# Twelve post-norms in PSUM, diagonals on ScalarE, and three small reorderings between the layers of a two-block fp32 network

## The reference, cut to what matters

```python
# block 1: stages 0, 1, 2 - the output y is normed ahead of the addition
x = x + 0.5 * rms_norm(swiglu_ffn(rms_norm(x, norm_pre[0]), ...), norm_post[0])
x = x + rms_norm(token_mixer(rms_norm(x, norm_pre[1]), ...), norm_post[1])
x = x + 0.5 * rms_norm(swiglu_ffn(rms_norm(x, norm_pre[2]), ...), norm_post[2])
# block 2: stages 3, 4, 5 - y is added as it is
h = h + 0.5 * swiglu(rms_norm_2(h, ffn1_norm), ...)
h = h + merged @ w_out
h = h + 0.5 * swiglu(rms_norm_2(h, ffn2_norm), ...)
```

## Time and profile before

| | |
|---|---|
| median of three runs | 2366.21 us (2357.22 to 2366.54) |
| the profiled execution | 2365.65 us, of which its span is 2364.3 us |
| TensorE matmuls busy | 2299.1 us |
| TensorE weight loads busy | 1890.1 us |
| GpSimd busy | 1317.9 us |
| VectorE busy | 868.7 us |
| ScalarE busy | 448.2 us |

### The profile page before, as it was taken

How to read it: one execution, slowest core, us unless ns; L and a number is a source line. 1 busy time by engine, 2 the same in 40 slices (tenths; PEclk the granted TensorE clock), 3 DMA queues, 4 the chain that set the end, 5 groups by cost and what they waited for, 6 DMA issues and landing times.

```text
span 2364.3 us, 25758 instructions
## 1 busy us (share of the span) xinstructions
PE 2299.1 (97%) x10888; PEld 1890.1 (80%) x10888; DVE 868.7 (37%) x902; ACT 448.2 (19%) x721; POOL 1317.9 (56%) x772
## 2 busy tenths in 40 slices
PE   8999998999999999999999999999988999999999
PEld 7888887887778888888888888877656788888887
DVE  3333104884234434104543202321567623434013
ACT  3111003323223111003111002011268121111012
POOL 5666664634146666665666665656114656666654
PEclk9999999999799999999999999999899999999999
DMA  4333332211123333332323332233000223333322
GB/s 177 98 98 94 94 97 72 73 53 54 36 80 96 93 98 98 98 98 82 98 95 95 96 98 90 89 92 98 27 1 1 72 89 98 98 96 94 105 89 89
DMA packets 55579, 201.04 MB, mean 85 GB/s; under 512 B 6408, under 2 KB 6536, under 8 KB 55336
## 3 DMA queue, kind: packets, MB, share of 16 engines
q1 hardware_dynamic: 53856, 194.14, 26.6%
q10 hardware_dynamic: 1608, 5.25, 0.6%
HBM read 197.27 MB, written 2.10 MB: 84 GB/s over the span
## 4 chain that ended last, share of the span: by engine, by line
PE 90%; DVE 5%; ACT 3%; issue 2%; POOL 1%; DMA 0%; ACTq 0%; DVEq 0%; POOLq 0%
PE psum L385 19%; PE psum L386 19%; PE psum L387 19%; PE psum L466 7%; PE psum L468 7%; PE psum L467 7%; PE psum L611 1%; DVE x L1722 1%; PE psum L1106 1%; PE psum L666 1%; PE psum L1108 1%; PE psum L1107 1%; PE psum L504 1%; PE psum L948 1%; ACT work L1567 1%
## 5 line engine op out<-in xcount | busy, mean ns | idle before, releaser
L350 POOL TENSOR_TENSOR w_lo<-w_raw,w_hi 128x1024 fp32r<-128x1024 f32 (+1 forms) x365 | 885.7, 2427 | 30.4
L348 POOL TENSOR_SCALAR w_hi<-w_raw 128x1024 fp32r<-128x1024 f32 (+1 forms) x365 | 391.1, 1072 | 889.2 <-PE psum L387 641.9
L385 PE MATMUL psum<-u_hi,w_hi 128*128 128x512 f32 (+1 forms) x2072 | 795.5, 384 | 4.3 <-DVE u_lo L1682 2.2
L386 PE MATMUL psum<-u_hi,w_lo 128*128 128x512 f32 (+1 forms) x2072 | 790.5, 382 | 0.0
L387 PE MATMUL psum<-u_lo,w_hi 128*128 128x512 f32 (+1 forms) x2072 | 790.4, 381 | 0.0
L385 PEld LDWEIGHTS psum<-u_hi,w_hi 128*128 128x128 f32 x2072 | 393.6, 190 | 82.2 <-issue 4.8
L387 PEld LDWEIGHTS psum<-u_lo,w_hi 128*128 128x128 f32 x2072 | 393.5, 190 | 74.4
L386 PEld LDWEIGHTS psum<-u_hi,w_lo 128*128 128x128 f32 x2072 | 393.8, 190 | 73.7 <-issue 0.7
L466 PE MATMUL psum<-w_hi,hidden_hi 128*128 128x512 f32 x800 | 311.7, 390 | 1.0 <-DVE work L1945 1.0
L467 PE MATMUL psum<-w_lo,hidden_hi 128*128 128x512 f32 x800 | 311.2, 389 | 0.0
L468 PE MATMUL psum<-w_hi,hidden_lo 128*128 128x512 f32 x768 | 298.8, 389 | 0.0
(11 more groups left out here) (280 smaller groups left out, 1716.1 us busy)
## 6 DMA issues: line engine op xcount, KB each, us to landing
w_raw<-in_ffn_in SPq DMA_DIRECT2D x176, 512.0 KB, 3.5
w_raw<-in_ffn_out SPq DMA_DIRECT2D x88, 512.0 KB, 3.5
w_raw<-in_proj_in SPq DMA_DIRECT2D x34, 512.0 KB, 3.5
w_raw<-in_mix_in SPq DMA_DIRECT2D x29, 512.0 KB, 3.5
w_raw<-in_embed SPq DMA_DIRECT2D x10, 512.0 KB, 3.6
w_raw<-in_mix_out SPq DMA_DIRECT2D x8, 512.0 KB, 3.5
w_raw<-in_branch SPq DMA_DIRECT2D x8, 512.0 KB, 3.5
w_raw<-in_proj_out SPq DMA_DIRECT2D x8, 512.0 KB, 3.5
```

Source lines behind the costliest of these rows:

```text
L348: pool.tensor_scalar(hi, raw, 1.0, 1.0, ALU.mult, ALU.mult).then_inc(k.w_split, 1)
L350: pool.tensor_tensor(lo, raw, hi.bitcast(F32), ALU.subtract).then_inc(k.w_split, 1)
L385: pe.matmul(out, hi[:, cols], xhi, start=first, stop=False)
L386: pe.matmul(out, lo[:, cols], xhi, start=False, stop=False)
```

## The change

Five things are done.

1. The post writes its product back to the PSUM banks that it read; the update reads PSUM. The two scratch buffers are no longer used there, and the wait on them is gone. Since `y` now lies in PSUM until the update, turning waits for `x_updated` in every stage.
2. In front of the gated mixer ScalarE builds the four diagonals (new `act_diag`); VectorE keeps the inverse.
3. There, VectorE's update 1 moves ahead of tile 0's inverse, and post 2 and update 2 both stand ahead of tile 1's inverse.
4. In stages 4, 5 and 6 ScalarE squares the fourth tile of `x` behind both pairs' roundings.
5. In stage 0 TensorE turns tile 2 ahead of the first chunk.

```diff
 def wait_out_taken(k, eng, st, i):
-    if st < 3:
-        eng.wait_ge(k.t_done, NT * st + i + 1)
-    else:
-        eng.wait_ge(k.x_updated, NT * st + i + 1)
+    eng.wait_ge(k.x_updated, NT * st + i + 1)
...
     pe_turn_tile(k, s, 0)
     pe_turn_tile(k, s, 1)
+    pe_turn_tile(k, s, 2)
     if s == 0:
         pe_dense_half(k, s, name, c0, CHUNK_BANK[0], 0)
-    pe_turn_tile(k, s, 2)
     pe_turn_tile(k, s, 3)
...
+def act_diag(k, i):
+
+    act = k.nc.scalar
+    act.wait_ge(k.x_inv, i + 1)
+    act.activation(k.diag[:, i * P:(i + 1) * P], k.cst(C_ID), ACT.Copy, scale=k.x_r[:, i:i + 1]).then_inc(k.x_diag, 1)
...
         square_y(2)
+        if s not in LATE:
+            act_diag(k, 0)
         square_x(1)
         square_y(3)
+        if s not in LATE:
+            act_diag(k, 1)
         square_x(2)
+        if s not in LATE:
+            act_diag(k, 2)
+            square_x(3)
+            act_diag(k, 3)
     else:
-        for i in range(NT):
+        for i in range(NT - 1):
             square_x(i)
-    if s not in LATE:
-        square_x(3)
     act_hi(k, s, 0)
     act_hi(k, s, 1)
     if s in LATE:
-        if st < 3:
-            square_x(3)
+        square_x(3)
...
     dve.reciprocal(r, r).then_inc(k.x_inv, 1)
-    dve.wait_ge(k.x_inv, i + 1)
-    dve.tensor_scalar(k.diag[:, i * P:(i + 1) * P], k.cst(C_ID), r, None, ALU.mult).then_inc(k.x_diag, 1)
...
-    if i >= 2:
-        dve.wait_ge(k.x_updated, NT * st + i - 1)
-    elif i == 0:
+    if i == 0:
         dve.wait_ge(k.post_loaded, 16 * (st + 1))
     scale = factors(k, st)[:, i:i + 1] if st in LATE else 1.0
-    dve.scalar_tensor_tensor(out=t, in0=y, scalar=scale, in1=k.post[:, :], op0=ALU.mult, op1=ALU.mult).then_inc(k.t_done, 1)
+    dve.scalar_tensor_tensor(out=y, in0=y, scalar=scale, in1=k.post[:, :], op0=ALU.mult, op1=ALU.mult).then_inc(k.t_done, 1)
...
-        dve.scalar_tensor_tensor(out=x, in0=normed_tile(k, i), scalar=r, in1=x, op0=ALU.mult, op1=ALU.add).then_inc(k.x_updated, 1)
+        dve.scalar_tensor_tensor(out=x, in0=out_tile(k, i), scalar=r, in1=x, op0=ALU.mult, op1=ALU.add).then_inc(k.x_updated, 1)
...
         dve_update(k, st, 0)
+        dve_update(k, st, 1)
         if s not in LATE:
             dve_root_x(k, s, 0)
-        dve_update(k, st, 1)
         dve_post(k, st, 2)
+        dve_update(k, st, 2)
         if s not in LATE:
             dve_root_x(k, s, 1)
-        dve_update(k, st, 2)
```

More of the change, by code:

```diff
@@ L1696, in dve_post @@
 def dve_post(k, st, i):
-    dve, t, y = k.nc.vector, normed_tile(k, i), out_tile(k, i)
+    dve, y = k.nc.vector, out_tile(k, i)
     dve.wait_ge(k.y_squared, NT * st + i + 1)
-    if i >= 2:
-        dve.wait_ge(k.x_updated, NT * st + i - 1)
-    elif i == 0:
+    if i == 0:
         dve.wait_ge(k.post_loaded, 16 * (st + 1))
     scale = factors(k, st)[:, i:i + 1] if st in LATE else 1.0
-    dve.scalar_tensor_tensor(out=t, in0=y, scalar=scale, in1=k.post[:, :], op0=ALU.mult, op1=ALU.mult).then_inc(k.t_done, 1)
-def normed_tile(k, i):
-    return k.scf[:, (1 + 2 * (i % 2)) * T:(3 + 2 * (i % 2)) * T]
+    dve.scalar_tensor_tensor(out=y, in0=y, scalar=scale, in1=k.post[:, :], op0=ALU.mult, op1=ALU.mult).then_inc(k.t_done, 1)
 def dve_update(k, st, i):
```

## The result

The changed kernel takes **2345.65 us** (median of 7 executions, 2343.45 to 2346.74). Beside it, seven executions of the kernel before had a median of 2357.22 us (2355.15 to 2366.54). The ratio is 0.9935, with a 95% interval of 0.9918 to 0.9953: 0.65% faster (the means of the seven are 2360.0 and 2345.2). A second set on another chip gave 2345.47 us and 0.9931 [0.9910, 0.9952]. The profiled execution took 2346.0 us, its span 2344.7 us, at a mean granted clock of 0.987. The one before took 2365.65 us, at 0.982.

A forecast was written before the change was run, and what follows sets the result against it. TensorE was held to bound the kernel, so only seams, where it waits for VectorE, could win. Gains of 8.5 + 2.0 + 1.8 + 1.9 + 1.1 = 15.3 us from 2365.65 gave 2350 us, range 2342 to 2362.

The forecast's parts named there:

- the base of the sum: Whole kernel: the profiled execution, 2365.65 us, from which the gains were subtracted, held to lie 0.6 us under the runs' median.
- rival A: Mixers and later work: shifted half-clock stretches eat part of the gain, 5 us, giving 2362 us; chance 0.12.
- better ends: Seams and start: the largest gains allowed for the five terms, 8.8 + 4 + 3 + 2 + 2 us.
- The start: Start of the program: tile 2's eight transposes fit into TensorE's idle 2.23 us, gaining 1.1 us, ends 0 and 2.
- Seam 2: Between stages 1 and 2: update 3 ends sooner, so the first chunk comes 2.0 us earlier, ends 1.1 and 4.
- Seam 1: Ahead of the gated mixer (stage 1): first chunk 8.5 us earlier, low end 5.6 if TensorE drops to half clock.
- Seam 3: Between stages 2 and 3: update 3 ends sooner, so the first chunk comes 1.8 us earlier, ends 0.8 and 3.
- Seams 4, 5, 6: Starts of stages 4, 5 and 6: ScalarE's rounding begins sooner, 3 x 0.6 = 1.9 us as written, ends 1.2 and 2.
- Post in PSUM: VectorE's post at the seams: reading and writing PSUM takes 1.28 us, upper bound 2.56 us, a gain excluded.
- rivals B and C: First three seams: PSUM post takes 2.56 us, giving 2361 us (chance 0.07), or 3.37 us, giving 2371 us (chance 0.03).
- Diagonal on ScalarE: Ahead of the gated mixer: each diagonal built on ScalarE takes 0.3 us, bounds nothing and 0.41 us.
- Rival D: Ahead of the gated mixer: ScalarE's four waits for the inverse cost 1 us each, giving 2354 us; chance 0.08.

The follow-up runs named there:

- e6_in_place_shift: Kernel before with post and update in PSUM alone, plus eight unused matmuls ahead of the attention mixer's 32nd projection chunk: 2356.18 us, ratio 0.9981.
- e8_after_shift: Changed kernel plus eight unused matmuls ahead of the attention mixer's 32nd projection chunk: median 2346.01 us, ratio 0.9940; its traced execution took 2355.97 us.

## Why the prediction was right on the seams and wrong in size

Forecast 2350 us, measured 2345.65: 4.4 us too high. As a gain it is further off: 2350 lies 7.2 us under the median of the kernel before, and 11.6 were measured (the ratio of 0.9935 says 15).

- **The step that failed is the base of the sum**, "the profiled execution lies 0.6 us under the median of the runs". The three executions then known were 2366.21, 2366.54 and 2357.22 us, and their spread of 9 us was given no term. With seven the median is 2357.22, 8.4 us under the profiled execution. Of 91 executions of the kernel before whose clock is on record above, 33 were at 0.982 or 0.983 (2364 to 2367 us), 29 at 0.985 or 0.986 (2358 to 2362) and 29 at 0.987 (2355 to 2358). The sum was subtracted from the slowest of these groups. The trace of the changed kernel lies 19.7 us under that one, with the mixers' half clock alike in both.
- **That the time came near is luck in part.** From the median of 2357.22 the sum of 15.3 would have given 2341.9 us, 3.7 below the measured time. A base 8.4 us too high and a sum above the 11.6 us between the medians went against each other. The medians lie closer than the traces because the median execution of the kernel before has less half clock in it than the traced one, and the changed kernel has stayed within 3.3 us of time.
- **The sum has no term for the mixers.** Against the trace at 0.986 the start, the seams and stages 2 and 3 gave 17.0 us, 1.7 more than the sum, and the mixers took 4.56 back. The prediction has this only as its rival A.
- **The range** names its better ends, 8.8 + 4 + 3 + 2 + 2 = 19.8 us, which give 2345.85 us. The measured time lies 0.2 us below that. The range's lower end of 2342 is nearly 4 us lower still, and no term stands for these.
- **Two terms were too small against the same trace, both by the clock.** The start was taken at 1.1 us and gave 3.0, since a half-clock stretch behind TensorE's idle 2.23 us went away with it. Seam 2 was taken at 2.0: the seam gave 2.50 and the layer behind it 1.84, as the half clock of its first chunks (0.56 us a row, 0.37 after) went away; the prediction had that as its upper end ("the first chunk is faster too", 4 us). It wasn't the wait that decided it, which is as long as before (2.20 us against 2.12); behind a wait of 2.21 us, the kernel `e6_in_place_shift` turned there at half clock, 16 in 3.28 us, and seam and layer together gained 2.7 us there instead of 4.3. These two are 4.2 of the 4.3 us between the sum of 15.3 and the 19.6 of the ledger's left column.
- **Seam 1 was right**: 8.64 measured against the same trace, 8.5 taken (7.67 against the trace at 0.986). The replay's end fits to 0.15 us (first post to chunk 16.85 forecast, 17.00 measured), and update 3 ends 377.25 + 1.29 - 366.05 = 12.5 us behind the first post, as replayed. The full clock held there, which was the better end.
- **Seam 3**: taken 1.8, measured 1.06, and 1.72 with the layer. Update 3 came 2.5 us sooner, as forecast, but TensorE turned at half clock, 16 in 3.17 us. That was the low end, 0.8.
- **Seams 4, 5, 6**: 0.61, 0.55, 0.60, together 1.76. The prediction took 3 x 0.6 and wrote 1.9, which should be 1.8.
- **Post in PSUM**: 1.29 us, taken 1.28. With it rivals B and C fell.
- **Diagonal on ScalarE**: rows of 0.39 us, taken 0.3, bound 0.41. The next instruction starts 0.29 us behind it (372.98 to 373.27), so in the replay 0.3 was the right step. The estimate from the Trainium skill (VectorE: DVE Perf Modes, section on the TRN2 errata), 0.29 us, fits that step and not the row. Rival D fell: ScalarE waited 0.83 and 0.23 us for an inverse, where it had nothing else to do.
- **The dearer PSUM source of the Trainium skill** (VectorE: DVE Perf Modes, same section; 120 cycles against 58) again showed no step: 1283 ns from SBUF without GpSimd beside it, 1283 ns from PSUM.
- **Rival A**, the mixers' clock taking back part, was priced at 5 us with a chance of 0.12. The half-clock stretches it names are real, and differ between executions: they cost the traced execution with the post in PSUM alone 7.65 us in stage 4, and the changed kernel 4.56 against the traces at 0.986. It didn't show against the trace that served as the base, since that had lost as much. That the change itself brings them on is not shown. A half-clock microsecond costs 0.5 us: from 0.9825 to 0.987 of 2360 us are 2 x 0.0045 x 2360 = 21 us at half clock, and the groups lie 10 us apart.

What stays open: why the changed kernel has kept within 3.3 us so far and the kernel before spreads over 12, and what in the mixers decides it. Neither the moment of the start nor 1 to 2 us of work moved it in a way that could be foretold.

## What to carry to other kernels

Before subtracting a sum from a traced execution, see where that execution stands among the others by its mean granted clock. Between two kernels compare stretch by stretch, and first those that the change leaves alone: an equal mean clock doesn't say that they had equal half clock there. An instruction of VectorE with two SBUF inputs took up to 2.1 us more than its 1.28 us beside a busy GpSimd; leaving one operand in PSUM took that away and cost 9 ns. Give each seam a term of its own for the half clock that may stand behind it: it was worth 1.7 us at the start and 1.8 in the layer behind seam 2, as much as the work removed.

## What the runs showed of the hardware

- A VectorE instruction that reads and writes the same PSUM banks costs 1292 ns for 128x1024, against 1284 into SBUF.
- The contention goes both ways: beside the long update GpSimd's rounding took 2.02 us, in seam 1 of the changed kernel, beside VectorE's PSUM forms, 1.04 to 1.05. A 128x128 product takes VectorE 0.29 us alone and up to 1.90 beside GpSimd.
- The same program on the same chip has several levels of time, 2355 to 2367 us. The traces at 2358 and 2366 us differ by half-clock stretches inside work that is otherwise the same. The mean granted clock of an execution, 0.982 to 0.987 for the kernel before, tells its time within 3 us. The Trainium skill (TensorE: Matmul & The Clock Gate, section "What's actually happening") says of a kernel's first matmuls that their slow part varies from run to run, and puts its price under 1% of a typical span. Here, away from the start for the most part, the levels lie up to 0.4% apart, nearly as much as the change.
- In the attention mixer alone the time at 1.2 GHz was 20.5 us in one traced execution (`e6_in_place_shift`) and 54.6 in another (`e8_after_shift`), with the same matmuls of TensorE in the same order.
